# GpSimd builds all matrices of a blocked S5 recurrence, the first quarter of them during the input product before it

## The reference, cut to what matters

```python
def layer_c(x, norm_g, w_in, lam_re, lam_im, log_step, b_re, b_im, c_re, c_im, d, glu_w, glu_b, w_out):
    h = rms_norm(x, norm_g)
    u, gate = jnp.split(h @ w_in, 2, axis=-1)
    y = s5_ssm(u, lam_re, lam_im, log_step, b_re, b_im, c_re, c_im, d).astype(x.dtype)
    z = jax.nn.gelu(y)
    z = z * jax.nn.sigmoid(z @ glu_w + glu_b)
    return x + (z * jax.nn.silu(gate)) @ w_out
# s5_ssm: groups of 16 channels share a 64-wide complex diagonal state:
#   x_t = L x_{t-1} + B u_t ;  y_t = Re(C x_t) + D u_t
```

## Time and profile before

| what | us |
|---|---|
| runs, lowest / median / highest of 3 | 4315.87 / 4317.69 / 4322.70 |
| the profiled execution's own time | 4310.84 |
| its span | 4309.0 |
| `c_in` stream, first cast to last evacuation | about 3588 to 3781.5 |
| recurrence stage `s5_blocks` | 3781.5 to 4086.2 |
| the products after it | 4086.2 to 4309.0 |

### The profile page before, as it was taken

One profiled execution on the slowest core, in us unless ns is written; L12 is line 12 of the kernel. 1 busy time (PEld: TensorE's weight loads), 2 busy tenths in 40 slices (PEclk: granted clock), 3 DMA queues, 4 the chain that ended last, 5 costly groups with the idle time before them and its releaser, 6 DMA issues. The chain is left out here.

```text
span 4309.0 us, 45587 instructions
## 1 busy us (share of the span) xinstructions
PE 3402.2 (79%) x17184; PEld 2472.0 (57%) x17184; DVE 2385.3 (55%) x3216; ACT 1197.9 (28%) x1863; POOL 920.0 (21%) x737
## 2 busy tenths in 40 slices
PE   6899997466999837777777777769996687957598
PEld 1688675346999833323333333339874486945498
DVE  6564314656875476566565565424435345477664
ACT  0332122333433411111111111024433233444642
POOL 0000002101000036545546555300002000042210
PEclk9899998677999969999999999989997598976699
DMA  8475222005965459999999999925540044500053
GB/s 335 170 291 191 81 83 68 5 2 192 367 228 174 142 212 424 427 427 428 428 427 428 428 427 428 427 113 194 189 151 11 22 144 141 171 15 6 14 191 127
DMA packets 176522, 940.28 MB, mean 218 GB/s; under 512 B 21870, under 2 KB 27246, under 8 KB 98068
## 3 DMA queue, kind: packets, MB, share of 16 engines
q0 software_dynamic: 82944, 604.02, 33.9%
q1 hardware_dynamic: 93468, 334.90, 22.8%
HBM read 936.75 MB, written 2.10 MB: 218 GB/s over the span
## 5 line engine op out<-in xcount | busy, mean ns | idle before, releaser
L1416 PE MATMUL bank<-pe_v_rows,pe_diag 128*128 128x512 f32 x2048 | 957.0, 617 | 345.0 <-DMA pe_v_rows<-in_expert_v,pe_staged_v 202.6
L1416 PEld LDWEIGHTS bank<-pe_v_rows,pe_diag 128*128 128x128 f32 x2048 | 385.3, 195 | 916.1 <-issue 599.8
L1314 DVE SCALAR_TENSOR_TENSOR pe_junk<-pe_u_rows,h_rows 128x2048 f32<-128x2048 f32 x256 | 586.8, 2292 | 444.1 <-DMA pe_u_rows<-in_expert_u,pe_staged_u 433.0
L1258 POOL DMA_INDIRECT pe_v_rows<-in_expert_v,pe_staged_v x256 | 322.6, 1260 | 348.7 <-PE bank L1416 287.2
L1258 POOL DMA_INDIRECT pe_u_rows<-in_expert_u,pe_staged_u x256 | 345.4, 1349 | 229.4 <-DVE pe_junk L1314 146.2
L245 PE MATMUL bank<-h_parts,b_top 128*128 128x256 f32 x2048 | 370.9, 284 | 9.0 <-DVE b_rest L342 9.0
L245 PEld LDWEIGHTS bank<-h_parts,b_top 128*128 128x128 f32 x2048 | 320.9, 193 | 10.0 <-DVE b_rest L342 9.3
L342 DVE TENSOR_TENSOR in_rest<-in_ring,in_top 128x1024 fp32r<-128x1024 f32 x112 | 137.1, 1225 | 324.0 <-ACT in_top L315 323.9
L1384 ACT ACTIVATE pe_diag<-ident,pe_weights 128x128 f32<-128x128 f32 x256 | 97.8, 399 | 773.9 <-PE bank L1416 768.1
L245 PE MATMUL bank<-h_parts,b_rest 128*128 128x256 f32 x1024 | 290.4, 284 | 0.0
L245 PE MATMUL bank<-h_parts,in_top 128*128 128x256 f32 (+1 forms) x1024 | 254.5, 340 | 14.2 <-DVE in_rest L342 14.2
(11 more groups left out here) (478 smaller groups left out, 6976.8 us busy)
## 6 DMA issues: line engine op xcount, KB each, us to landing
b_ring<-in_w_mix SPq DMA_DIRECT2D x128, 512.0 KB, 5.7
in_ring<-in_w_in SPq DMA_DIRECT2D x112, 512.0 KB, 3.7
ab_ring<-in_w_ab SPq DMA_DIRECT2D x112, 512.0 KB, 4.5
mod_ring<-in_w_mod SPq DMA_DIRECT2D x32, 1024.0 KB, 6.7
v_rows<-in_w_mod POOLq DMA_DIRECT2D x32, 1024.0 KB, 5.6
k_cols<-in_w_mod POOLq DMA_DIRECT2D x32, 1024.0 KB, 8.0
c_ring<-in_w_c_in SPq DMA_DIRECT2D x64, 512.0 KB, 3.6
c_ring<-in_w_glu_out SPq DMA_DIRECT2D x64, 512.0 KB, 4.6
```

Source lines behind the costliest of these rows:

```text
L1258: gp.indirect_dma_start(buf[:, slot, :], None, table, bass.IndirectOffsetOnAxis(ap=staged[which][:, tile, e:e + 1], axis=0)).then_inc(sems ...
L1314: nc.vector.scalar_tensor_tensor(out=junk[:, :], in0=ub[:, s, :], scalar=1.0, in1=h2tm[:, tile, :], op0=ALU.mult, op1=ALU.mult, accum_out= ...
L1416: mm = nc.tensor.matmul(banks[4 * tile + b][:, :], diag[:, e % 4, :], vb[:, s, b * 512:(b + 1) * 512], start=False, stop=False, skip_group ...
```

## The change

A new class `S5Rows` owns `gt`, two `h` buffers, the raw buffers and two scratch tiles, and builds both kinds of rows with GpSimd instructions; `SplitAndPrepare` is a hook that makes quarter 0's drive and read rows on POOL while the `c_in` stream runs (its raw DMA is issued by SP in front of half unit 8). To make room, the `c_in` ring has 3 slots instead of 4. In `s5_blocks` POOL then builds drive rows and read rows of quarters 1 to 3; DVE keeps only three smaller memsets, `skip` and `scan`. The within-group matmuls of four neighbouring pairs write to the four groups of 32 partitions of one bank, a quarter to a bank; `within` is signalled once per quarter, `diag` and `eye` span 128 partitions, and ACT's 16 copies to `m` come after the whole quarter, and after `put(q)` instead of ahead of it.

```diff
+class S5Rows:
+    C = 16
+    def product(self, link, q, steps, table, rows, out, op):
+        nc, C, pairs = self.nc, self.C, slice(q * QP, (q + 1) * QP)
+        p1, p2 = self.b1[:, :, 0:steps, :], self.b2[:, :, 0:steps, :]
+        for p, (k, n) in zip((p1, p2), rows):
+            row = self.raw[q % 2][:, :, k, :].unsqueeze(2).broadcast_to([P, QP, steps, C])
+            by = table[:, n, :, pairs].rearrange("p s q -> p q s").unsqueeze(3).broadcast_to([P, QP, steps, C])
+            link(nc.gpsimd.tensor_tensor(p, row, by, ALU.mult))
+        for rows, cols in self.own_group:
+            ins = nc.gpsimd.tensor_tensor(out[rows, :, :, cols], p1[rows], p2[rows], op)
+            link(ins)
+    def drive(self, link, q):
+        table = self.tables[0]
+        self.product(link, q, STEP, table, ((0, 0), (1, 1)), self.gt[:, :, 0], ALU.subtract)
+        self.product(link, q, STEP, table, ((0, 1), (1, 0)), self.gt[:, :, 1], ALU.add)
+    def read(self, link, q):
+        table = self.tables[1]
+        self.product(link, q, STEP + 1, table, ((2, 0), (3, 1)), self.h[q % 2][:, :, 0], ALU.subtract)
+        self.product(link, q, STEP + 1, table, ((2, 2), (3, 3)), self.h[q % 2][:, :, 1], ALU.add)
+
+class SplitAndPrepare(SplitFirst):
+    uses_gp = True
+    def sp_step(self, sp, h):
+        if h == 8:
+            sp.dma_start(self.rows.raw[0][:, :, :, :], self.t["s5_bc"][:, 0:QP, :, :]).then_inc(self.raw_in, 16)
+    def gp(self, gp):
+        link = Chain(gp, self.prepared)
+        link(self.nc.gpsimd.memset(self.rows.gt[:, :, :, :, :], 0.0))
+        link(self.nc.gpsimd.memset(self.rows.h[0][:, :, :, :, :], 0.0))
+        gp.wait_ge(self.raw_in, 16)
+        self.rows.drive(link, 0)
+        self.rows.read(link, 0)
...
         def _(sp):
+            sp.dma_start(rows.raw[1][:, :, :, :], t["s5_bc"][:, pairs(1), :, :]).then_inc(raw_in[1], 16)
+            sp.dma_start(rows.raw[0][:, :, :, :], t["s5_bc"][:, pairs(2), :, :]).then_inc(raw_in[0], 16)
             sp.dma_start(dcol[:, :], t["s5_d"]).then_inc(d_in, 16)
...
+            sp.dma_start(eye[:, :], t["c_eye"]).then_inc(d_in, 16)
+            sp.wait_ge(gt_done, 1)
+            sp.wait_ge(h_done, 1)
+            sp.dma_start(rows.raw[1][:, :, :, :], t["s5_bc"][:, pairs(3), :, :]).then_inc(raw_in[1], 16)
...
         def _(gp):
             link = Chain(gp, gchain)
...
+            for q in range(1, NQ):
+                gp.wait_ge(raw_in[q % 2], 16 * ((q + 1) // 2))
+                gp.wait_ge(turned, 8 * q)
+                gp.wait_ge(within, q)
+                rows.drive(link, q)
+                gp.sem_inc(gt_done, 1)
+                if q == 1:
+                    gp.wait_ge(zeroed, 3)
+                else:
+                    gp.wait_ge(y_done, 2 * (q - 1))
+                rows.read(link, q)
+                gp.sem_inc(h_done, 1)
...
             def kernels(q):
-                pe.wait_ge(h_done, 2 * (q + 1))
+                if q >= 1:
+                    pe.wait_ge(h_done, q)
                 pe.wait_ge(d_done, q + 1)
...
+                if q >= 2:
+                    pe.wait_ge(m_out, 16 * (q - 1))
+                for c in range(4):
+                    for r in range(4):
+                        out = banks[2 + q % 2][32 * r:32 * r + 32, c * P:(c + 1) * P]
                         for s in range(2):
...
+                            nc.tensor.matmul(out, gt[:, 4 * c + r, s, STEP - 1, :], rows.h[q % 2][:, 4 * c + r, s, 0:STEP, :].rearrange("p s c -> p (s c)"), start=(s == 0), stop=False)
+                        mm = nc.tensor.matmul(out, diag[32 * r:32 * r + 32, q % 2, c, :], eye[32 * r:32 * r + 32, :], start=False, stop=True)
+                mm.then_inc(within, 1)
...
+                act.wait_ge(within, q + 1)
+                for r, s in stack:
+                    src = banks[2 + q % 2][32 * r:32 * r + 32, :].rearrange("p (q c) -> p q c", q=4)
+                    nc.scalar.activation(m[32 * s:32 * s + 32, q % 2, r::4, 32 * s:], src[:, :, 0:P - 32 * s], ACT.Copy).then_inc(m_out, 1)
...
+                put(q)
+                if q + 1 < NQ:
                     take_m(q + 1)
-                put(q)
...
-            nc.vector.memset(h[:, :, :, :, :, :], 0.0).then_inc(zeroed, 1)
+            nc.vector.memset(x[:, :, 0, :, :, 0], 0.0).then_inc(zeroed, 1)
             nc.vector.memset(m[:, :, :, :], 0.0).then_inc(zeroed, 1)
+            nc.vector.memset(rows.h[1][:, :, :, :, :], 0.0).then_inc(zeroed, 1)
...
             skip(0)
-            read_rows(0)
+            skip(1)
             for q in range(NQ):
                 scan(q)
-                if q + 1 < NQ:
-                    skip(q + 1)
-                    read_rows(q + 1)
+                if q + 2 < NQ:
+                    skip(q + 2)
...
-                dict(kind="fm", n=16, cols=T, rhs=lambda s, k: h[s][:, k, :], evac=gate_out)], stream_buffers(sb, "c", s1), banks,
-                SplitFirst(nc, "c_in", h4, *h))
+                dict(kind="fm", n=16, cols=T, rhs=lambda s, k: h[s][:, k, :], evac=gate_out)], stream_buffers(sb, "c", s1, slots=3), banks,
+                SplitAndPrepare(nc, t, "c_in", h4, *h, s5_rows))
```

More of the change, by code:

```diff
@@ L2010, in _, with __init__ @@
             link(nc.vector.tensor_single_scalar(read[:, 2:4, :, :], read[:, 1::-1, :, :], -1.0, ALU.mult))
-def s5_blocks(st, nc, t, banks, u, tables, con):
+class S5Rows:
+    C = 16
+    def __init__(self, nc, sb, tables):
+        self.nc, self.tables = nc, tables
+        self.gt = sb("s5_drive_t", [P, QP, 2, STEP, 32])
+        self.h = [sb("s5_read_0", [P, QP, 2, STEP + 1, 32]), None]
+        self.raw = [sb("s5_raw_0", [P, QP, 4, self.C]), None]
+        self.b1, self.b2 = sb("s5_b1", [P, QP, STEP + 1, self.C]), sb("s5_b2", [P, QP, STEP + 1, self.C])
+        self.own_group = [(slice(64 * k, 64 * k + 64), slice(self.C * k, self.C * k + self.C)) for k in range(2)]
+    def product(self, link, q, steps, table, rows, out, op):
[16 more added lines that the diff above has]
+        self.product(link, q, STEP + 1, table, ((2, 2), (3, 3)), self.h[q % 2][:, :, 1], ALU.add)
@@ new lines, with __init__, bind @@
+class SplitAndPrepare(SplitFirst):
+    uses_gp = True
+    def __init__(self, nc, t, name, source, high, low, rows):
+        super().__init__(nc, name, source, high, low)
+        self.nc, self.t, self.rows = nc, t, rows
+    def bind(self, sem, segments):
+        super().bind(sem, segments)
+        self.raw_in, self.prepared = sem("s5_first_raw_in"), sem("s5_first_prepared")
+    def sp_step(self, sp, h):
[8 more added lines that the diff above has]
+        self.rows.read(link, 0)
@@ L2017, in s5_blocks @@
+def s5_blocks(st, nc, t, banks, u, tables, rows, con):
     with ExitStack() as own, st.stage() as (block, sem):
@@ L2022, in s5_blocks @@
         leap, leap_swing = leaps[:, ::2], leaps[:, 1:]
[L2023 to L2026, removed]
+        gt = rows.gt
+        rows.h[1], rows.raw[1] = sb("read_1", [P, QP, 2, STEP + 1, 32]), sb("raw_1", [P, QP, 4, rows.C])
+        dcol = sb("d", [P, KT])
+        eye = sb("eye", [P, P])
+        diag = sb("skip", [P, 2, 4, 32])
         g = sb("drive", [P, QP, 2, P])
-        h = sb("read", [P, 2, QP, 2, STEP + 1, 32])
         m = sb("within", [P, 2, QP, P])
@@ L2031, in s5_blocks @@
         x = sb("x", [P, 2, ROWS + 1, 2, QP, COLS])
-        b1, b2 = sb("b1", [P, QP, STEP + 1, C]), sb("b2", [P, QP, STEP + 1, C])
-        p1, p2 = sb("p1", [P, QP, STEP, C]), sb("p2", [P, QP, STEP, C])
         m1, m2 = sb("m1", [P, 2, QP, COLS]), sb("m2", [P, 2, QP, COLS])
-        diag = sb("skip", [32, QP, 32])
         raw_in = [sem("ss_raw_in0"), sem("ss_raw_in1")]
-        d_in, cleared, zeroed, chain, gchain = sem("ss_d_in"), sem("ss_cleared"), sem("ss_zeroed"), sem("ss_chain"), sem("ss_gchain")
+        d_in, zeroed, chain, gchain = sem("ss_d_in"), sem("ss_zeroed"), sem("ss_chain"), sem("ss_gchain")
         gt_done, turned, g_out = sem("ss_gt_done"), sem("ss_turned"), sem("ss_g_out")
@@ L2041, in s5_blocks @@
         scanned, y_done, z_out, d_done = sem("ss_scanned"), sem("ss_y_done"), sem("ss_z_out"), sem("ss_d_done")
-        own_group = [(slice(64 * k, 64 * k + 64), slice(C * k, C * k + C)) for k in range(2)]
         stack = [(r, s) for r in range(4) for s in range(STEP)]
@@ L2084, in turn @@
             def turn(q):
[L2085 removed]
+                if q >= 1:
+                    pe.wait_ge(gt_done, q)
                 for n in range(8):
@@ L2127, in outputs @@
                         for s in range(2):
-                            mm = nc.tensor.matmul(out.rearrange("p (i b) -> p i b", b=COLS), h[:, q % 2, k, s, 1:, :].rearrange("p s c -> p (s c)"), x[:, q % 2, 0:ROWS, s, k, :],
+                            mm = nc.tensor.matmul(out.rearrange("p (i b) -> p i b", b=COLS), rows.h[q % 2][:, k, s, 1:, :].rearrange("p s c -> p (s c)"), x[:, q % 2, 0:ROWS, s, k, :],
                                                   start=False, stop=(s == 1))
@@ L2201, in _, with skip @@
```

(12 more changed lines are left out.)

16 lines of the change are left out of this document (4 added, 12 removed).

## The result

The changed kernel's median is 4345.84 us (4340.84 to 4349.52) beside 4317.44 before: 28.4 us more, a ratio of 1.006 (95% interval 1.0043 to 1.0076). Slower was forecast, 4336.2 with 4304 to 4352. On another chip it came out the same: 4341.9 beside 4313.3, 1.007 (1.0046 to 1.0095).

The account below looks back on a forecast made before the run. PE bounds `c_in`; a chain of waits bounds the recurrence. Recurrence +16.5 and `c_in` +2 make +18.5 us on the profiled 4310.84: 4329.3, or 4336.2 for the median; own range 4322 to 4349, full range 4304 to 4352.

Parts of the forecast that it names:

- (a): Recurrence start: quarter 0's matrices are ready, so `take_g(0)` follows `take_u(0)` and scan 0 starts 19.7 us earlier.
- (b): kernels(0): 14.2 us as before, within 15% either way; a pair's three products still follow one another into the same partitions.
- (d): Scan 0: POOL's 39.6 us of rows stretch it to 67.6 us, eating the whole gain of the earlier start.
- (e): outputs(0) and kernels(1): after a long PE pause they take 20.5 and 24.9 us.
- (f): Before scan 2: drive rows 2 take 18.1 us for 27.8, so scan 2 starts 10.0 us earlier.
- (g): Scan 2: POOL's rows 2 and 3 add 5.4 and 32.9 us to its 32.0, ending it 13.1 us late.
- (h): outputs(2), kernels(3): a 14 us PE pause halves the clock, copies to `m` follow, and the stage ends 16.5 us later.
- B: Rival, 0.20: PE keeps full clock in outputs(2) and kernels(3); no change, 4316.4 us.
- (i): `c_in`: POOL's turns with DVE cost 2 us, between nothing and 7; three ring slots cost nothing.
- Rival C: Chance 0.10: slower by more, `c_in` stalls with each turn of DVE and POOL, 7 us for 2; 4341 or up to 4349.
- D: Rival dismissed without a chance: POOL finishes quarter 0's rows late and the recurrence waits for it.
- Rival A: Chance 0.12: column groups work at once, kernels take a quarter of the time, and the median falls to 4297 us.

Follow-up runs that it names:

- `a_busy2`: Changed kernel plus 76 extra products into a free bank ahead of outputs(2); recurrence stage 304.5 us, ratio 1.0039 to the kernel before.
- `b_ring3`: Kernel before with the `c_in` ring cut from four slots to three, run once for its profile; ACT's waits for the ring's DMA 9.5 us.
- `a_inter`: Changed kernel with the within-group products of four pairs interleaved; recurrence stage 286.3 us, ratio 0.9979 to the kernel before.
- `best_dve_busy`: Changed kernel, products interleaved, four ring slots, quarters 1 to 3's drive and read rows on DVE, 78 extra products ahead of outputs(3); ratio 0.9874 to kernel before.

## Why the prediction was right

The direction was right, and so was the mechanism; the size was 18.5 us forecast for 28.4 in the medians. The two stages that the change touches give 26.1 of these, and the rest lies within the interval (some 19 to 33 us). The profiled execution came out 38.7 later, but 15.3 of that is the chance part ahead of `c_in`. By steps:

(a), (b), (c): scan 0 started 24.6 us into the stage (24.9 forecast), kernels(0) took 14.2, drive rows 18.0 for 18.1. Read rows took 22.0 for 21.5: 5.07 and 5.88 for the pairs of 1280 elements.

(d) Scan 0 took 68.0, forecast 67.6: the 20 us won at the start were given back whole.

(e), (f) outputs(0) and kernels(1) 20.7 and 24.9, at half clock, as forecast; scan 2 started 171.3 us into the stage, forecast 170.9.

(g) Scan 2 took 73.3, forecast 70.3, the one term of the recurrence mis-sized. Its two meetings with GpSimd lasted 7.5 and 40.7 us (6.7 and 39.6 forecast), and of the 17 scan instructions beside the second six were short ones of 0.22, where I had counted 16 long ones.

(h) The pause was 17.4 us (14 forecast, as scan 2 ended later than I had it), and behind it outputs(2), kernels(3) and the copies took 20.7, 24.9 and 7.2, as forecast; `a_busy2` shows that the clock was the reason. B is out: the pause came, and cost the clock.

(i) `c_in` is the other mis-sized term: 5.7 for 2. The 2 rested on a subtraction seldom meeting the start of a GpSimd instruction. From the third on each was held up: 16 subtractions took 53.3 us, PE uses them up in 46.1, and of the 7.2 short PE waited 3.9, so the lead covered 3.3, not 6.3. The step also said that three slots cost nothing, and `b_ring3` bears that out for the ring alone. But it took the two edits one by one, the lead for the ring without GpSimd's turns. Rival C, 7 for `c_in`, was nearer than the forecast (5.7, and 6.4 in the second profile), and the median lies in its 4341 to 4349; 3.9 of the way there are the recurrence's, not C's.

D is out as well: GpSimd was done with quarter 0 at 3679.8, 123 us ahead of the stage.

Rival A was wrong for this order of products and right for another: `a_inter` shows the fourfold rate. The "against" stands as written, that a pair's three products follow one another into the same partitions. Of the two rules of the Trainium skill, TensorEngine Tiling's "up to 4x" (Theoretical Speedup) agrees with `a_inter`, 14.2 us to 3.8, once neighbours differ; the drain at a change of mode (Key Properties) is shown by no run: the same edit cut the changes from 8 to 2 in twelve products, and what they cost was not measured apart. Two changes in twelve left nearly the fourfold rate; an order with other neighbours and still eight changes was not run, so what the eight would cost there is open.

## What to carry to other kernels

An engine with idle time is not free to use: if its instructions hold up those of the engine that others wait for, moved work can cost more than it did there. Between GpSimd and DVE here the bill was the moved span, less one DVE instruction for each moved one. When a step is moved earlier, look what PE loses: work that used to follow dense products may now follow a pause. For column groups, the order of the instructions decides, not the layout alone.

## What was not expected

- A pause of 0.61 us (`a_busy2`) left the clock at 1.00; one of 0.94 us (`best_dve_busy`) dropped it to 0.50 for the 20.7 us of outputs(3) behind it. Before each PE had been busy for some 30 us or more. The 3.25 us of the kernel before still show 1.00, and the fall to 0.51 comes behind them; how long a pause it takes is not shown.
- With interleaved products kernels(1) ran at a mean clock of 0.70 behind outputs(0) at 0.50, so the clock rose inside 5 us; in the old order it never rose in 24.9:

```profile
3891.40:3912.10 20.70, 20.67 (x100) 0.50 0.01 2
3912.10:3917.20 5.10, 5.05 (x97) 0.70 0.00 0
```

- Ahead of the changed part the same instructions took between 3575 and 3609 us from one profile to the next, more than the whole effect of the change.
